# A diffusion step on one NeuronCore: the first modulation loads regrouped by column, the projection's weight in three loads

## What is computed

```python
def ada_modulation(cond, w, b):
    m = jax.nn.silu(cond) @ w + b
    return jnp.split(m, 6, axis=-1)
...
    sh1, sc1, g1, sh2, sc2, g2 = ada_modulation(c_ctx, w_ada[l], b_ada[l])
    h = rms_norm(xp, norm1_g[l]) * (1.0 + sc1) + sh1
    q, k, v, u_pool, u_conv = input_projection(h, w_in[l])
...
    s_loc = jnp.einsum('brchd,brjkhd->bhrcjk', qg, kg).astype(jnp.float32) * scale + bias.astype(jnp.float32)
```

## Time and profile before

| what | value |
|---|---|
| median of three runs | 722.83 us |
| the profiled execution | 721.98 us |
| its span (first to last instruction) | 720.1 us |
| mean granted clock of TensorE | 0.992 |
| PE busy | 682.2 us, 95% |
| DVE, ACT, POOL busy | 232.1, 148.1, 149.6 us |
| read from memory, written | 163.13 MB, 22.31 MB |

### The profile page before, as it was taken

How to read it: one execution, slowest core, us unless ns; L and a number is a source line. 1 busy time by engine, 2 the same in 40 slices (tenths; PEclk the granted TensorE clock), 3 DMA queues, 4 the chain that set the end, 5 groups by cost and what they waited for, 6 DMA issues and landing times.

```text
span 720.1 us, 12047 instructions
## 1 busy us (share of the span) xinstructions
PE 682.2 (95%) x5015; PEld 406.3 (56%) x5015; DVE 232.1 (32%) x512; ACT 148.1 (21%) x323; POOL 149.6 (21%) x182
## 2 busy tenths in 40 slices
PE   3899999999999999999899999999999999999894
PEld 2557646465457775544585455566546655654551
DVE  4310099900325763333486010110111011110137
ACT  6112101101256662121310010111101110111102
POOL 5137930900043531213111000000000000000050
PEclk9999999999999999999999999999999999999997
DMA  9994750609967333380655989799999999994183
GB/s 326 388 318 74 235 224 3 232 1 377 279 235 262 119 118 119 125 342 29 218 221 188 329 295 392 276 391 403 373 390 414 403 377 420 395 412 155 47 292 146
DMA packets 50824, 186.19 MB, mean 259 GB/s; under 512 B 7184, under 2 KB 9737, under 8 KB 46544
## 3 DMA queue, kind: packets, MB, share of 16 engines
q1 hardware_dynamic: 43568, 163.18, 60.6%
q0 software_dynamic: 7088, 22.17, 9.2%
q10 hardware_dynamic: 112, 0.04, 0.0%
HBM read 163.13 MB, written 22.31 MB: 258 GB/s over the span
## 4 chain that ended last, share of the span: by engine, by line
PE 87%; DMA 6%; DVE 4%; issue 1%; ACT 1%; SPq 0%; POOL 0%; DVEq 0%; ACTq 0%; POOLq 0%
PE bank L1814 12%; PE bank L1526 12%; PE bank L1821 10%; PE bank L1650 10%; PE bank L1837 6%; PE bank L1846 5%; PE bank L1589 5%; DMA slots<-in_w_ada 4%; PE bank L1471 3%; PE bank L1531 3%; PE bank L1829 3%; PE bank L1487 3%; PE bank L1684 2%; PE bank L1801 2%; PE bank L1854 2%
## 5 line engine op out<-in xcount | busy, mean ns | idle before, releaser
L1526 PE MATMUL bank<-ra,slots 128*128 128x512 f32 x192 | 83.3, 594 | 0.4 <-DVE ra L893 0.4
L1650 PE MATMUL bank<-slots,rc 128*128 128x512 f32 x160 | 69.9, 593 | 0.0
L1220 DVE TENSOR_TENSOR rc<-re,bank 128x256 f32<-128x256 f32 (+1 forms) x32 | 10.2, 359 | 160.6 <-PE bank L1821 88.3
L1526 PEld LDWEIGHTS bank<-ra,slots 128*128 128x128 f32 x192 | 36.1, 190 | 45.6 <-issue 44.6
L1414 POOL COPY gi<-ridx 128x1 uint32<-128x1 uint32 x16 | 3.0, 185 | 258.2 <-PE bank L1801 237.6
L1814 PE MATMUL bank<-rb,rc 128*128 128x512 f32 x128 | 56.2, 595 | 0.0
L570 ACT ACTIVATE rb<-bank 128x512 f32<-128x512 f32 (+1 forms) x64 | 30.3, 524 | 112.9 <-PE bank L1526 49.7
L908 DVE SCALAR_TENSOR_TENSOR re<-re,cwT 128x670 f32<-128x670 f32 x60 | 52.3, 948 | 0.0
L1650 PEld LDWEIGHTS bank<-slots,rc 128*128 128x128 f32 x160 | 29.9, 190 | 34.9 <-issue 34.9
L1305 POOL TENSOR_TENSOR mod<-mod,vecT 128x8 f32<-128x8 f32 (+1 forms) x8 | 19.6, 2455 | 122.8 <-ACT mod L570 122.8
L1821 PE MATMUL bank<-slots,rc 128*64 128x256 f32 x384 | 43.6, 381 | 0.0
(11 more groups left out here) (299 smaller groups left out, 987.2 us busy)
## 6 DMA issues: line engine op xcount, KB each, us to landing
slots<-in_w_ada SPq DMA_DIRECT2D x12, 2048.0 KB, 14.1
slots<-in_moe_w_gate SPq DMA_DIRECT2D x8, 2048.0 KB, 11.2
rb<-in_moe_w_gate SPq DMA_DIRECT2D x8, 2048.0 KB, 11.3
rb<-in_moe_w_up SPq DMA_DIRECT2D x8, 2048.0 KB, 12.9
rb<-in_moe_w_down SPq DMA_DIRECT2D x8, 2048.0 KB, 10.4
slots<-in_moe_w_up SPq DMA_DIRECT2D x8, 2048.0 KB, 12.5
slots<-in_moe_w_down SPq DMA_DIRECT2D x8, 2048.0 KB, 13.3
scratch_yd<-rb SPq DMA_DIRECT2D x1, 7680.0 KB, 21.3
```

The source lines that it names most:

```text
L1526: ins = mm(b[:, :], w[:, k, m * P:(m + 1) * P], hT[:, k, 0:NLAT], start=k == 0, stop=k == KD - 1)
L1650: ins = mm(b[:, :], mT[:, k, i * P:(i + 1) * P], wo[k // 4][:, k % 4, 512 * hf:512 * hf + 512], start=k == 4, stop=k == 3)
```

## The change

- **Columns.** The first four modulation blocks now hold 256 columns of the shift and the same 256 of the scale. Block j gives both for slices 2j and 2j + 1. The load is two loads of 1 MB, shift half and scale half, each on a semaphore of its own. The matmuls of `ada` are the same. The blocks run 0, 1, 2, 3.
- **Projection weight.** The weight of block 3 comes in three loads: slices 0 and 1 behind block 0's load, 2 and 3 behind block 1's, 4 to 7 behind block 2's. It has its buffer (2) from the start; before it came behind block 2's load, as two loads, slices 0 and 1 and then the rest.
- **PE.** `adT(0)` stands between the last two tiles of activations. Then three rounds: all products of slice 2j - 2, `ada(j)`, half of those of slice 2j - 1, `adT(j)`, the other half. `cw` comes behind them. Slices 6 and 7 go output piece by output piece.
- **POOL and DVE.** POOL modulates shift and scale of two slices at a time, four times; its clearing of `re` stands behind the first. DVE waits for POOL at every second slice; its copy of `cw` goes behind the eighth.
- **SP.** The remaining constants are issued before `("in", 4)` and not before `("ada", 1)`.

The core of the diff:

```diff
-    plan += turned[0:6] + [(("ada", 0), "A")] + turned[6:] + [(("adT", 0), "A"), (("ada", 2), "A"), (("adT", 2), "A")]
+    plan += turned[0:6] + [(("ada", 0), "A")] + turned[6:8] + [(("adT", 0), "A")] + turned[8:]
+    for j in (1, 2, 3):
+        plan += [(("ada", j), "A"), (("adT", j), "A")]
     plan += [(("cw",), "D")]
...
-ORDER = [("ada", 0), ("ada", 2), ("in", 3), ("ada", 1), ("ada", 3), ("in", 4), ("ada", 4), ("ada", 5), ("in", 0),
+ORDER = [("ada", 0), ("in", 3), ("ada", 1), ("ada", 2), ("ada", 3), ("in", 4), ("ada", 4), ("ada", 5), ("in", 0),
...
-SLOT = [0, 1, 2, 0, 1, 0, 1, 2, 1, 0, 2, 1, 0, 2, 1, 0, 2, 1, 0]
+SLOT = [0, 2, 1, 0, 1, 0, 1, 2, 1, 0, 2, 1, 0, 2, 1, 0, 2, 1, 0]
...
+            if kind == "ada" and j < 4:
+                src = t["w_ada"][0].rearrange("(k p) (v n) -> p k v n", p=P, v=6)[:, :, 0:2, 256 * j:256 * j + 256]
+                dst = slots[:, SLOT[n], :].rearrange("p (k v n) -> p k v n", k=KD, v=2)
+                sp.dma_start(dst[:, :, 0, :], src[:, :, 0, :]).then_inc(shift_in[j % 2], 16)
+                sp.dma_start(dst[:, :, 1, :], src[:, :, 1, :]).then_inc(w_slot[SLOT[n]], 16)
+                if j in (1, 2):
+                    ks = slice(2, 4) if j == 1 else slice(4, KD)
...
+                    sp.dma_start(dst, src).then_inc(S["w3_next"] if j == 1 else w_slot[SLOT[1]], 16)
+                continue
...
-        for a in (0, 4):
-            modulation(0, a, 4)
-            modulation(1, a, 4)
+        for a in range(0, KD, 2):
+            modulation(0, a, 2)
+            modulation(1, a, 2)
+            if a == 0:
+                filled(pool, "xT", TT - 1, 1)
+                g.memset(re[:, 0:e0], 0.0).then_inc(S["pads_ready"], 1)
...
-        begin(0, range(4))
-        begin(1, range(4))
-        ada(1)
-        slot("in", 3)
-        begin(2, range(4))
-        adT(1)
-        ada(3)
-        begin(3, range(2))
-        adT(3)
-        begin(3, range(2, 4))
-        project(3, "pa", "pac", begun=4)
+        for j in range(1, 4):
+            if j == 2:
+                pe.wait_ge(S["w3_next"], 16)
+            if j == 3:
+                slot("in", 3)
+            begin(2 * j - 2, range(4))
+            ada(j)
+            begin(2 * j - 1, range(2))
+            adT(j)
+            begin(2 * j - 1, range(2, 4))
...
+        project(3, "pa", "pac", begun=6)
```

More of the change, by code:

```diff
@@ L186 @@
 NTH = {key: n for n, (key, _) in enumerate(PLAN)}
-ASIDE = {("table",): 5, ("ada", 1): 6, ("adT", 1): 7, ("ada", 3): 6, ("adT", 3): 7}
+ASIDE = {("table",): 5, ("cw",): 6}
+ASIDE.update({(kind, j): n for j in (1, 2, 3) for kind, n in (("ada", 6), ("adT", 7))})
 ASIDE.update({("S", u): u % 4 for u in range(2 * PAIRS)})
@@ L314, in build @@
     rw = re[:, 5120:5440]
-    S = {n: sem(n) for n in """cst_in rest_in w3_in vec_in cw_in small_in poolw_in cachek_in cachev_in rpb_in rpad_out rwin_out raw_in bc_in bc2_in
+    S = {n: sem(n) for n in """cst_in rest_in w3_in w3_next vec_in cw_in small_in poolw_in cachek_in cachev_in rpb_in rpad_out rwin_out raw_in bc_in bc2_in
         psum_full evac_a evac_d cond_zero cond_ready ssq_ready ms_ready sqrt_ready xn_ready mod_ready h_ready h0_ready
@@ L326, in build @@
     w_odd = [sem(f"w_odd{i}") for i in range(3)]
+    shift_in = [sem(f"shift_in{i}") for i in range(2)]
     x_in = [sem(f"x_in{i}") for i in range(TT)]
@@ L427, in _ @@
                     sp.dma_start(x[:, 4, :], t["x_prompt"][0]).then_inc(x_in[4], 16)
-            if n == 3:
+            if n == 5:
                 sp.dma_start(cst[:, P:], t["consts"][:, P:]).then_inc(S["rest_in"], 16)
@@ L440, in _ @@
             kind, j = key
+            if kind == "ada" and j < 4:
[5 more added lines that the diff above has]
+                    ks = slice(2, 4) if j == 1 else slice(4, KD)
+                    src = t["w_in"][0].rearrange("(k p) n -> p k n", p=P)[:, ks, 512 * 3:512 * 4]
+                    dst = slots[:, SLOT[1], :].rearrange("p (k n) -> p k n", k=KD)[:, ks]
+                    sp.dma_start(dst, src).then_inc(S["w3_next"] if j == 1 else w_slot[SLOT[1]], 16)
+                continue
             if kind == "ada":
@@ L619, in ada @@
             if j:
-                filled(act, "adT", {2: 0, 1: 2, 3: 1}.get(j, j - 1))
+                filled(act, "adT", j - 1)
             b = filled(act, "ada", j)
@@ L625, in adT @@
             b = filled(act, "adT", j)
+            if j < 4:
+                evac(mod[:, 0:2, :, 2 * j:2 * j + 2], b[:, 0:P].rearrange("p (v k s) -> p v s k", v=2, k=2)[:, :, 0:2, :])
+                return
             evac(mod[:, j // 2, :, 4 * (j % 2):4 * (j % 2) + 4],
@@ L630, in _ @@
         xT(3)
+        adT(0)
         xT(4)
-        adT(0)
-        for j in (2, 1, 3):
+        for j in (1, 2, 3):
             ada(j)
@@ L883, in _ @@
         xT(4)
-        b = filled(dve, "cw")
-        evac(cwT[:, :], b[:, 0:NCW])
         emptied(dve, "xT", TT - 1, 0)
@@ L889, in _ @@
         for k in range(KD):
-            if k % 4 == 0:
-                dve.wait_ge(S["mod_ready"], k // 2 + 2)
+            if k % 2 == 0:
+                dve.wait_ge(S["mod_ready"], k + 2)
             for s, (a, n) in ((1, (0, NLAT)), (0, (NLAT, NTOK))):
@@ L895, in _ @@
             ins.then_inc(S["h_ready"], 1)
+        b = filled(dve, "cw")
+        evac(cwT[:, :], b[:, 0:NCW])
         emptied(dve, "cw")
@@ L1294, in _ @@
         pool.dma_start(t["rpad"], rprow[0:120, :]).then_inc(S["rpad_out"], 16)
-        filled(pool, "xT", TT - 1, 1)
-        g.memset(re[:, 0:e0], 0.0).then_inc(S["pads_ready"], 1)
         def modulation(vec, a=0, n=KD):
-            emptied(pool, "adT", 2 * vec + (a + n) // 4 - 1)
+            emptied(pool, "adT", a // 2 if vec < 2 else 2 * vec + 1)
             m = mod[:, vec, :, a:a + n]
@@ L1481, in ada @@
             w = slot("ada", j).rearrange("p (k n) -> p k n", k=KD)
+            if j < 4:
+                pe.wait_ge(shift_in[j % 2], 16 * (j // 2 + 1))
             if j == 0:
@@ L1507, in _ @@
                 ada(0)
[L1509 to L1514, removed]
+            if i == 3:
+                adT(0)
         def project(load, latent, prompt, width=512, begun=0):
@@ L1538, in _ @@
         keep_warm(10)
-        emptied(pe, "cw")
-        emptied(pe, "adT", 2)
+        emptied(pe, "adT", 0)
+        emptied(pe, "xT", TT - 1, 0)
+        emptied(pe, "xT", TT - 1, 1)
         def begin(k, ms):
@@ L1545, in begin @@
                 mm(bank[BANK["pa", m]][:, :], w3[:, k, m * P:(m + 1) * P], hT[:, k, 0:NLAT], start=k == 0, stop=False)
-        begin(0, range(4))
-        begin(1, range(4))
-        ada(1)
-        slot("in", 3)
-        begin(2, range(4))
-        adT(1)
-        ada(3)
-        begin(3, range(2))
-        adT(3)
-        begin(3, range(2, 4))
-        project(3, "pa", "pac", begun=4)
+        for j in range(1, 4):
[8 more added lines that the diff above has]
+            begin(2 * j - 1, range(2, 4))
+        pe.wait_ge(S["cw_in"], 16 * (len(VR2) + 1))
+        b = take("cw")
+        give(nc.tensor.transpose(b[:, 0:NCW], cwrow[0:NCW, :], ident[0:NCW, 0:NCW]))
+        project(3, "pa", "pac", begun=6)
         ada(4)
@@ L1627, in modT @@
         def modT():
-            pe.wait_ge(S["mod_ready"], 8)
+            pe.wait_ge(S["mod_ready"], 12)
             b = take("modT")
```

3 lines of the change are left out of this document (removed).

## The result

The change makes the kernel slower, by 4.2 us at the medians.

The account below looks back on a forecast made before the run. TensorE bounds the kernel, with 87% of the chain of waits. A gain of 0.89 us by the prompt part and a 0.83 us wait for query weights sum to -0.06: 722.8 us at the median, range 721.2 to 724.6.

Parts of the forecast that it names:

- The opening: Up to the first projection product: one 2 MB load in halves replaces two waits; start at 24.0, 3.9 us earlier.
- The rounds: Three rounds of the first projection block: 9.79 us each, ending 0.6 to 0.8 us late behind POOL and DVE.
- Rival (b): Rounds hide their POOL and DVE chain and the weight loads suffer less: 1.76 us gained, 721.1; chance 0.17.
- The gain up to the prompt part: First projection block: its prompt part starts at 60.28 instead of 61.17, a gain of 0.89 us.
- The windows' start: POOL's queue: it starts 4.55 us later, so its sixteen position-bias window loads go out from 62.4.
- 5.44 x 0.074 = 0.403 MB take 6.2 us, in which the loads lose 79%: Windows beside weight loads: 4.9 us lost against 4.07 of slack, so 0.83 us of wait at the query projection.
- rival (c): Windows start later and slide further into the loads, query weights landing after 91.2; 2 us later gives 724.6; chance 0.15.
- The Trainium skill's turns: Queues alternating by packet leave the loads 0.146 MB a us and no query-weight wait, sum -0.89; set aside for the trace.
- That the two nearly cancel is no accident: Gain 0.89 against wait 0.83: query weights land at about 89.7 however early the first block ends.

Follow-up runs that it names:

- before_late: The kernel before the change, with POOL's position-bias window writes and loads moved behind its pooling branch: 722.51 us, ratio 1.0003 to before.
- before_delayed: The kernel before the change, with POOL waiting for the second result of the first projection block ahead of its window writes: 726.61 us, ratio 1.005.
- late_adt1: late_windows with each round's transposed modulation behind one product of the odd slice instead of two: 719.61 us, ratio 0.9949 to before.
- late_windows: The changed kernel with POOL's position-bias window writes and loads moved behind its pooling branch: 722.46 us, ratio 0.9994 to before.
- diagonal: The changed kernel, transposed modulation behind one product, windows in their old place but in 23 loads, each into every ninth partition: 721.62 us, ratio 0.9993 to before.
- alternate: The changed kernel with the sixteen window loads issued to lower and upper half of the partitions in turn: 726.55 us, ratio 1.0053 to before.
- aligned: The changed kernel with each window load reading from a start that is a multiple of 128 elements: 727.8 us, ratio 1.0067 to before.
- elsewhere: The changed kernel with the window loads reading rows of the modulation weight instead of the scratch tensor: 728.33 us, ratio 1.0078 to before.
- warm_wait: The changed kernel with thirteen identity matmuls ahead of the query projection: 724.94 us, ratio 1.0037 to before.
- spread: The changed kernel with each window load's eight rows put into every eighth partition, not eight side by side: 722.09 us, ratio 0.9987 to before.

## Why the prediction was wrong, point by point

- **The opening** came out near, first product at 23.65 for 24.01, but in part by luck: two errors offset each other. The first block was complete at 16.92 for 17.76, although loads of 1 KB rows ran slower than taken (356 GB/s over 14 to 25, not 375). The 17.58 in before, from which 17.76 was worked out, is late: before_late and before_delayed, with the same opening, have 16.99 and 16.45. Against that, transpose to first product took 3.91 us (19.74 to 23.65) where 2.54 + 0.29 + 0.5 = 3.33 were priced, so that the chain of POOL and DVE ended last, with 0.53 us of wait, and not TensorE's own row.
- **The rounds** were right: 9.80 us for 9.79, waits of 0.50, 0.50 and 0.43 for the 0.6 to 0.8 forecast. Here too two small errors cancel: the first eight instructions took 3.60 us for 3.45 (23.65 to 27.25), and transpose to next round 2.49 for 2.64 (30.96 to 33.45). Rival (b), rounds without a wait, was out; late_adt1 shows that it took one product less in front.
- **The gain up to the prompt part** was 1.18 for 0.89. In late_windows it was 0.94, and all of that reached the query projection.
- **The windows' start** was right: 62.62 for 62.4.
- **The step that failed** is the term "5.44 x 0.074 = 0.403 MB take 6.2 us, in which the loads lose 79%", a wait of 0.83. It was 3.24. The mechanism and the place are those forecast; the rates of the earlier trace rows did not hold. They come from 2 us of a short overlap in before. In after the first 2 us of the overlap were much the same, DMA view of 68 to 70:

```profile
q0 software_dynamic: 42, 0.16, 52.4%
q1 hardware_dynamic: 68, 0.14, 35.4%
```

But then the windows had only 0.09 MB over 70 to 74, and over 75 to 82 0.047 MB a us for the 0.065 assumed. So the two queues ran together from 67.3 to about 82, and the query weights took 22.6 us to landing for the 20 forecast. They landed at 91.87, past the 91.2 that rival (c) named, but by the pace of the windows beside the loads and not by a later start as (c) had it.
- **A term was missing**: the clock. The prediction let a wait cost its own length. Behind 3.24 us of idle TensorE the granted clock was 0.51 for 3.4 us, which cost 1.70. With the wait alone the time would have been 2.1 us above before, just past the range; this took it well past. The longer stretch at half clock at the gather, 1.27 in the profiled execution, is not shown to belong to the change.
- **The Trainium skill's turns** (DMA: Bandwidth & Descriptors, Queues, rings and completion order) would have given the loads 2.25 times the windows' bytes. I set that aside for the 1.2 of the earlier trace rows; over 75 to 82 it was 0.65 / 0.33 = 2.0, nearer to the rule than to my row. Its estimate of 0.146 MB a us for the loads and no wait did not come true all the same (0.093 and 3.24 us): the total fell to 0.14, of which the rule says nothing.
- **"That the two nearly cancel is no accident"** was wrong. They cancel only as long as the rates do not depend on how long the queues overlap.

## What to carry to other kernels

Before an engine's work moves, look at the transfers that stand behind it in program order, and at which large load they will then run beside; a price for that from two microseconds of an overlap need not hold for the rest of it (0.065 MB a us became 0.047 here). Price a wait of TensorE with what the clock may do behind it, here half as much again or more in four of the six profiled executions with an unfilled wait at the query projection. In this kernel, loads that put long rows into a few neighbouring partitions are best issued where no other queue has something due: moved there, with one product less ahead of each transpose, the same regrouping gains 3.3 us (719.61 against 722.94 beside it).

## What the runs showed of the hardware that was not expected

- **Neighbouring partitions.** Eight rows of 8 KB into eight partitions side by side went at 0.073 to 0.083 MB a us with three different sources, into every eighth partition at 0.13, POOL's own pace. What in the destination limits them the runs don't show.
- **The sum of two queues.** Weight loads alone move 0.386 MB a us; beside the windows both together moved 0.14 in after and 0.21 in diagonal, with the engines counted full. Why the total falls so far is open.
- **The clock behind a wait.** The fall behind the idle TensorE is not certain. In after, before_delayed, alternate and diagonal (2.42 to 3.32 us idle) the granted clock was 0.66 over five us from about the wait's end; in aligned (3.42) and elsewhere (2.58) it was 1.00, and the 64 instructions took 27.73. These two are among the executions whose clock had fallen in the opening (next point), and so is warm_wait's; the other four are not. Whether the one fall keeps off the other was not tried.
- **The clock in the opening.** In four of the ten profiled kernels with the new opening (warm_wait, aligned, elsewhere, spread) the granted clock fell to half at about 17 us, and the first product came at 25.3 and not 23.7 to 24.1. From the windows of spread and of after, the same stretch:

```profile
14.00:25.00 11.00, 8.85 (x109) 7.93 (x109) 7.17 (x12) 4.00 (x7) 1.99 (x5) 0.84 1.09 356
```

```profile
14.00:25.00 11.00, 8.64 (x112) 7.34 (x113) 7.86 (x14) 3.99 (x7) 1.99 (x5) 1.00 1.09 356
```

No experiment was made on it. It may be a part of the changed kernel's wide spread, 721.9 to 730.36.
